# Cached values by columns: the sample group's weighted values on VectorE and ScalarE instead of TensorE

## What is computed

```python
s = einsum('bshd,bsjhd->bshj', q, kg) * scale + bias     # kg: 256 cached keys and the new one
e = exp(s - max(s));  den = sum(e)
o = einsum('bshj,bsjhd->bshd', e, vg) / den              # vg: 256 cached values and the new one
```

## Time and profile before

| | |
|---|---|
| median of 3 runs | 2500.4 us (2497.42 to 2500.45) |
| the profiled execution | 2495.72 us |
| its span | 2494.2 us |
| TensorE busy | 99% of the span |
| VectorE, ScalarE, GpSimd busy | 70%, 38%, 10% |
| mean granted TensorE clock | 0.997 |

### The profile page before, as it was taken

How to read it: one execution, slowest core, us unless ns; L and a number is a source line. 1 busy time by engine, 2 the same in 40 slices (tenths; PEclk the granted TensorE clock), 3 DMA queues, 4 the chain that set the end, 5 groups by cost and what they waited for, 6 DMA issues and landing times.

```text
span 2494.2 us, 51724 instructions
## 1 busy us (share of the span) xinstructions
PE 2465.9 (99%) x20366; PEld 2450.5 (98%) x20366; DVE 1755.0 (70%) x2203; ACT 942.2 (38%) x1225; POOL 253.0 (10%) x281
## 2 busy tenths in 40 slices
PE   8999999999999999999999999999999999999998
PEld 7999999999999999999999999999999999999998
DVE  6777787778787899888888888888433332456332
ACT  5343334333433454444444444444322221233331
POOL 1120111011100000000000000000000000143000
PEclk9999999999999999999999999999999999999999
DMA  6353333333343334433333434343665543233331
GB/s 211 119 162 104 117 109 128 112 114 105 124 145 111 135 107 149 136 118 135 118 135 118 142 121 150 124 137 120 224 208 170 164 139 120 77 93 108 110 110 68
DMA packets 99741, 324.00 MB, mean 130 GB/s; under 512 B 18258, under 2 KB 18514, under 8 KB 99168
## 3 DMA queue, kind: packets, MB, share of 16 engines
q1 hardware_dynamic: 72144, 250.25, 30.3%
q0 software_dynamic: 26672, 70.69, 8.2%
q10 hardware_dynamic: 864, 2.24, 0.2%
HBM read 286.80 MB, written 40.65 MB: 131 GB/s over the span
## 4 chain that ended last, share of the span: by engine, by line
PE 92%; DVE 3%; DMA 2%; issue 1%; ACT 1%; SPq 0%; DVEq 0%; ACTq 0%
PE acc L566 17%; PE acc L570 17%; PE acc L568 17%; PE acc L769 12%; PE acc L770 12%; PE acc L768 12%; DMA wraw<-in_w_down 1%; PE aux L615 1%; PE aux L577 1%; DMA hid<-in_x_tiles 1%; PE aux L659 1%; DVE wlo L1268 1%; DMA wraw<-in_w_in 1%; PE aux L605 0%; ACT whi L909 0%
## 5 line engine op out<-in xcount | busy, mean ns | idle before, releaser
L1268 DVE TENSOR_TENSOR wlo<-wraw,whi 128x1024 fp32r<-128x1024 f32 (+1 forms) x276 | 333.6, 1209 | 359.2 <-ACT whi L909 358.4
L909 ACT ACTIVATE whi<-wraw 128x1024 fp32r<-128x1024 f32 (+1 forms) x276 | 285.4, 1034 | 666.2 <-PE acc L570 593.2
L768 PE MATMUL acc<-xb_hi,whi 128*128 128x260 f32 x1228 | 348.3, 284 | 2.3 <-DVE xb_lo_t L1667 2.3
L770 PE MATMUL acc<-xa_hi,wlo 128*128 128x260 f32 x1228 | 349.1, 284 | 0.0
L769 PE MATMUL acc<-xa_lo,whi 128*128 128x260 f32 x1228 | 349.1, 284 | 0.0
L768 PE MATMUL acc<-xa_hi,whi 128*128 128x260 f32 x1228 | 347.4, 283 | 0.6 <-DVE wlo L1618 0.6
L770 PE MATMUL acc<-xb_hi,wlo 128*128 128x260 f32 x1228 | 347.7, 283 | 0.0
L566 PE MATMUL acc<-slots_a,whi 128*128 128x260 f32 x1536 | 312.9, 285 | 0.0
L570 PE MATMUL acc<-slots_a,wlo 128*128 128x260 f32 x1536 | 309.1, 283 | 0.0
L568 PE MATMUL acc<-slots_a,whi 128*128 128x260 f32 x1536 | 309.1, 283 | 0.0
L1085 ACT ACTIVATE whi<-wraw 128x1024 fp32r<-128x1024 f32 x176 | 186.3, 1058 | 225.0 <-PE acc L770 117.0
(11 more groups left out here) (305 smaller groups left out, 5076.9 us busy)
## 6 DMA issues: line engine op xcount, KB each, us to landing
wraw<-in_w_in SPq DMA_DIRECT2D x96, 512.0 KB, 3.6
blocks<-in_w_gate SPq DMA_DIRECT2D x88, 512.0 KB, 6.0
blocks<-in_w_up SPq DMA_DIRECT2D x88, 512.0 KB, 6.0
wraw<-in_w_down SPq DMA_DIRECT2D x48, 448.0 KB, 3.4
wraw<-in_w_out SPq DMA_DIRECT2D x32, 512.0 KB, 3.6
wraw<-in_w_ple_gate SPq DMA_DIRECT2D x32, 512.0 KB, 3.5
slots_b<-f_dram SPq DMA_DIRECT2D x28, 520.0 KB, 4.5
f_dram<-sig_t POOLq DMA_DIRECT2D x22, 520.0 KB, 3.2
```

What stands on the lines that cost most here:

```text
L768: mm(to, w_h, hi, start=p == 0, stop=False)
L770: return mm(to, w_l, hi, start=False, stop=p == KP2 - 1)
L909: on(whi[:, u % HILO, 0:width], wraw[:, u % RAW, 0:width], ACT.Copy).then_inc(s_whi, 1)
L1268: V.tensor_tensor(wlo[:, u % HILO, 0:width], wraw[:, u % RAW, 0:width], whi[:, u % HILO, 0:width].bitcast(F32), ALU.subtract).then_inc(s_w ...
```

## The change

The cached values are laid out on the host with channels on partitions (`in_cache_v`: channel, pair, token, position), and are loaded into a tile of 8 rows of 257 columns for each partition, whose last column takes the new value. The normed probabilities (16 rows of 257) are stored to DRAM and loaded back twice, each head's rows spread over its 64 partitions (`p_rows`). In step 10, at its end, VectorE multiplies the two tiles in one instruction (`sample_products`), and ScalarE sums each of the 8 rows straight into `hid` (`sample_sums`). TensorE's products and transposes of steps 7 and 9 fall away, and so do the small products, copies and sums on VectorE in steps 7, 8 and 10.

What moves with it: the key products and their sums stand one step later (2, 3 and 4 instead of 1, 2 and 3). `p_rows` shares its place with `skew`, so the next pair's `skew` is loaded once the products are done, and the next pair's keys once the sums are done. `o_low` has no tile of its own any more and uses `gate_t` (`v_t` for the last pair). ScalarE waits for the stored probabilities before it writes the keys' root over their tile. The queries' low parts stand ahead of the convolution's taps. Pair 7's products and sums stand in step 12 of the output projection.

```diff
-            if g == 7:                                       # TensorE
-                pe.wait_ge(s_row, 5 * a + 5)
-                mm(aux[:, BANK_D, KCACHE * 2 * DEC:(KCACHE + 1) * 2 * DEC], ones[0:2 * DEC, :], new_diag[:, :],
-                   start=True, stop=True)
-                for t in range(KCACHE):
-                    done = nc.tensor.transpose(aux[:, BANK_D, t * 2 * DEC:(t + 1) * 2 * DEC],
-                                               row[:, t * P:(t + 1) * P], ident[0:2 * DEC, 0:2 * DEC])
-                done.then_inc(s_str, 1)
-            if g == 9:
...
-                pe.wait_ge(s_wv, 3 * a + 3)
-                for b in range(DEC):
-                    done = mm(aux[:, BANK_D, b:b + 1], kv[:, KCACHE * b, :], ones[:, 0:1], start=True, stop=True)
-                done.then_inc(s_spv, 1)
...
+        def sample_sums(a):                                  # ScalarE
+            act.wait_ge(s_out, 3 * a + 2)
+            for b in range(DEC):
+                done = on(cached[:, b, :], cached[:, b, :], ACT.Copy, accum_out=hid[:, a, SEQ + b:SEQ + b + 1])
+            done.then_inc(s_out, 1)
...
                 if a is not None:                            # ScalarE, step 8, ahead of the keys' root
                     act.wait_ge(s_qk, 2 * j)
+                    act.wait_ge(d_p, 16 * a + 16)
                 root_of(qk_rstd, HD).then_inc(s_root, 1)
...
                 heads(j, a, g, last)                         # ScalarE, the loop over steps
+                if a is not None and g == 10:
+                    sample_sums(a)
...
-            if g == 7:                                       # VectorE
-                dve.wait_ge(s_str, 2 * a + 2)
-                V.tensor_copy(p_cols.rearrange("p t c -> p (t c)"), aux[:, BANK_D, 0:3 * 2 * DEC]).then_inc(s_pc, 1)
-                dve.wait_ge(s_pc, a + 1)
+            if g == 8:
                 dve.wait_ge(l_vc, 16 * a + 16)
-                for t in range(KCACHE):
-                    V.tensor_tensor(cached(t), cached(t), p_cols[:, t, :].rearrange("p (b e) -> p b e", b=DEC)
-                                    .unsqueeze(3).broadcast_to([P, DEC, 2, HD]), ALU.mult).then_inc(s_wv, 1)
-                dve.wait_ge(s_wv, 3 * a + 2)
-                V.tensor_tensor(cached(0), cached(0), cached(1), ALU.add).then_inc(s_wv, 1)
...
+                V.tensor_copy(cached[:, :, PAST], qkv_s[:, 2, :]).then_inc(s_out, 1)
+        def sample_products(a):
+            dve.wait_ge(l_p_rows, 32 * a + 32)
+            dve.wait_ge(s_out, 3 * a + 1)
+            V.tensor_tensor(cached[:, :, :], cached[:, :, :], p_rows[:, :, :], ALU.mult).then_inc(s_out, 1)
...
             if g == 10 and not last:                         # VectorE
                 v_lo(j)
+                q_lo(j)
                 conv_taps(j, a)
-                q_lo(j)
...
                 heads(j, a, g, last)                         # VectorE, the loop over steps
+                if a is not None and g == 10:
+                    sample_products(a)
...
-            pool.dma_start(kv[:, :, :], cache_v[0].rearrange("b (t p) h d -> p (b t) (h d)", p=P)[
-                :, :, bass.ts(a, P)]).then_inc(l_vc, 16)
+            pool.dma_start(cached[:, :, 0:PAST], cache_v[:, bass.ds(a, 1), :, :].squeeze(1)).then_inc(l_vc, 16)
+
+        def store_probs(a):
+            pool.wait_ge(s_row, 4 * a + 4)
+            apart()
+            pool.dma_start(p_dram[bass.ds(a, 1)].squeeze(0).rearrange("b e i -> (b e) i"), row[:, :]).then_inc(d_p, 16)
+
+        def load_probs(a):
+            pool.wait_ge(d_p, 16 * a + 16)
+            pool.wait_ge(s_biased, 8 * a + 8)
+            for e in range(2):
+                apart()
+                pool.dma_start(p_rows[e * HD:(e + 1) * HD, :, :],
+                               p_dram[bass.ds(a, 1), :, e, :].broadcast_to([HD, DEC, ROW_W])).then_inc(l_p_rows, 16)
...
-            pool.wait_ge(s_spv, a + 1)                       # GpSimd, attention(a)
+            store_probs(a)
+            load_probs(a)
+            if fresh:
+                store_skew(14, 16)
+                pool.wait_ge(d_skew, 16 * 4)
+            pool.wait_ge(s_out, 3 * a + 2)
             apart()
-            load_keys(a + 1)
-            if fresh:
-                store_skew(14, 16)
-            pool.wait_ge(s_biased, 8 * a + 8)
+            load_skew(a + 1)
+            pool.wait_ge(s_out, 3 * a + 3)
             apart()
-            if fresh:
-                pool.wait_ge(d_skew, 16 * 4)
-            load_skew(a + 1)
+            load_keys(a + 1)
             pool.wait_ge(s_o, 2 * a + 2)
-            pool.wait_ge(s_out, 4 * a + 4)
+            pool.wait_ge(s_out, 3 * a + 3)
             add_squares(acc_attn, hid[:, a, :], 4 * a + (SQ_X + 2))
```

More of the change, by code:

```diff
@@ L201, in build @@
     v_both = sb("v_both", [P, QB, 2, P], F32R, mix)
-    o_low = sb("o_low", [P, SEQ], scope=mix)
     u_t = sb("u_t", [P, 2 + T], scope=mix)
-    skew = sb("skew", [P, 2, SEQ], scope=mix)
+    p_rows = sb("p_rows", [P, DEC, ROW_W], scope=mix)
+    skew = p_rows.rearrange("p b i -> p (b i)")[:, 0:2 * SEQ].rearrange("p (e s) -> p e s", e=2)
     prob = sb("prob", [P, 2, SEQ], scope=mix)
@@ L208, in build @@
     stats = sb("stats", [P, 3], scope=mix)
-    kv = sb("kv", [P, DEC * KCACHE, P], scope=mix)
+    cached = sb("cached", [P, DEC, ROW_W], scope=mix)
+    kv = cached.rearrange("p b i -> p (b i)")[:, 0:DEC * PAST].rearrange("p (n f) -> p n f", f=P)
     qkv_s = sb("qkv_s", [P, 3, DEC], scope=mix)
@@ L269, in build, with o_low @@
     t_odd = tmp[:, 0:2, :].rearrange("p a t -> p (a t)").rearrange("p (n h) -> p n h", h=HALF)
+    def o_low(final):
+        return (v_t if final else gate_t)[:, 0:SEQ]
     def halves(tile):
@@ L913, in root_of, with attention @@
             return on(halves(tile[:, :]), aux_sum, ACT.Sqrt, bias=EPS, scale=1.0 / width)
-        def attention(a, g):
+        def attention(a, g, final=False):
             if 1 <= g <= 8:
@@ L925, in attention @@
                 e = (g - 5) // 4
+                if e == 0:
+                    if final:
+                        act.wait_ge(d_v, 16 * KA)
+                    else:
+                        act.wait_ge(s_conv, a + 1)
                 act.wait_ge(s_pv, 4 * a + 2 * (e + 1))
-                on(o_low[e * HD:(e + 1) * HD, :], aux[(1 - e) * HD:(2 - e) * HD, BANK_O, :], ACT.Copy).then_inc(s_olow, 1)
+                on(o_low(final)[e * HD:(e + 1) * HD, :], aux[(1 - e) * HD:(2 - e) * HD, BANK_O, :], ACT.Copy).then_inc(s_olow, 1)
             if g <= 7:
@@ L1053, in _ @@
             if 3 <= i <= PAIR_UNITS + 2:
-                attention(KA - 1, i - 3)
+                attention(KA - 1, i - 3, final=True)
+            if i == 12:
+                sample_sums(KA - 1)
             if i < KA - 1:
@@ L1289, in attention @@
                 dve.wait_ge(s_olow, 2 * a + e + 1)
-                V.tensor_tensor(hid[rows, a, 0:SEQ], aux[rows, BANK_O, :], o_low[rows, :], ALU.add).then_inc(s_o, 1)
+                V.tensor_tensor(hid[rows, a, 0:SEQ], aux[rows, BANK_O, :], o_low(final)[rows, :], ALU.add).then_inc(s_o, 1)
             if g <= 7:
@@ L1351, in attention @@
-            if g == 8:
-                V.tensor_tensor(out_s[:, :, :], qkv_s[:, 2, :].unsqueeze(2).broadcast_to([P, DEC, 2]),
-                                p_cols[:, KCACHE, :].rearrange("p (b e) -> p b e", b=DEC), ALU.mult).then_inc(s_out, 1)
[L1354 to L1358, removed]
-                V.tensor_tensor(out_s[:, :, :], out_s[:, :, :],
-                                aux[:, BANK_D, 0:DEC].unsqueeze(2).broadcast_to([P, DEC, 2]), ALU.add).then_inc(s_out, 1)
-                dve.wait_ge(s_out, 4 * a + 2)
-                for e in range(2):
-                    V.tensor_copy(hid[e * HD:(e + 1) * HD, a, SEQ:T], out_s[e * HD:(e + 1) * HD, :, e]).then_inc(s_out, 1)
@@ L1578, in _ @@
                 attention(KA - 1, i - 3, final=True)
+            if i == 12:
+                sample_products(KA - 1)
             if i < KA - 1 or i == 13:
@@ L2106, in laid_out @@
     weights["in_w_ple_proj"] = columns("w_ple_proj", PT * P)
-    return {**weights, "in_x_tiles": tiles(x), "in_p_tiles": tiles(p), "in_old_state": tiles(old),
+    values = np.ascontiguousarray(given["cache_v"][0].reshape(DEC, PAST, KA, 2, HD).transpose(3, 4, 2, 0, 1)
+                                  ).reshape(P, KA, DEC, PAST)
+    return {**weights, "in_cache_v": values, "in_x_tiles": tiles(x), "in_p_tiles": tiles(p), "in_old_state": tiles(old),
             "in_gains": np.ascontiguousarray(np.concatenate(rows).T)}
```

64 lines of the change are left out of this document (29 added, 35 removed).

## The result

The changed kernel takes 2536.95 us (median of 4 runs, 2536.41 to 2540.11), the kernel before 2498.91 us (median of 4 runs): a ratio of 1.0156, 95% interval 1.0144 to 1.0169. It is slower by 38 us. The profiled execution took 2540.11 us with a span of 2538.6 us, 44.4 us more than before by either measure. It is the slowest of its four, while the profiled execution before was as short as the fastest of the others, so the profiles differ by 6 us more than the medians.

A forecast was written before the change was run, and what follows sets the result against it. TensorE bounds the kernel, with a VectorE chain just in time behind it. Six turns at +7.2 us (+43.2), the seventh +4.7 and the last pair -1.5 give +46.4; predicted 2545 us, 8-in-10 range 2516 to 2566.

The forecast's parts named there:

- The likeliest case: VectorE's hand-off to ScalarE and back, with slow clock after each wait: 2545 us, own range 2529 to 2565; 64%.
- The second bound: In each turn, a 34.5 us chain on VectorE delivers the first probabilities only 0.05 us before TensorE takes them.
- What leaves VectorE: Steps 7 to 10: dropped small work and quieter taps bring VectorE to the end of step 10's old work 2.8 us earlier.
- What comes in: End of step 10: product 2.35 us, ScalarE's sums 3.5 us, then its split; VectorE's split starts 4.25 us later.
- Contention: GpSimd's moved squares run beside VectorE's splits and gate products, ahead of the next pair's first softmax: 0.9 us, ends 0 and 1.4.
- The clock: After each 7 us wait of TensorE the granted clock falls to 0.50, costing 2.5 us, ends 0 and 3.1.
- The seventh turn: At the convolution's output projection, VectorE's operand splits wait for ScalarE's copies behind the sums: +4.7 us, 1 of it clock.
- Covers: Row store, row loads, skew and key loads stay hidden; the skew by 2 us, the key load by over 5.
- B: Same hand-off to ScalarE and back, but the clock holds: 2529 us, from 2519 to 2539; 15%.
- D: A transfer ends last, skew or rows landing late behind the weights' loads: 3 us a turn for the skew, 2563 us; 8%.
- E: Gain and hand-off cancel, with VectorE's chain growing by 0.3 us: 2500 us; 5%.
- C: Faster, TensorE alone bounding turns: -18 us, 2482; needs VectorE's chain 1.8 us shorter, sign decided by growth under 0.45; 8%.

The follow-up runs named there:

- the kernel with both orders: Against the changed kernel: VectorE's long product put ahead of the convolution taps and ScalarE's sums behind its split of step 11; 2500.67 us, ratio 1.0007 against the kernel before.

## Why the prediction was right

The likeliest case held by its mechanism, with sizes a little too large: 2545 predicted, 2537 measured; on the footing of the profiled executions 2542 against 2540.1. The second agreement is partly luck: of the 44.4 us measured, 2.7 lie in the start stage, which the prediction did not have. Without them 41.7 us stand against the 46.4 predicted; by the medians it is 38.0.

- **The second bound.** Right. VectorE's chain sets the turn: when it was shortened step by step, the turn fell from 88.81 to 80.16 us, with the same work on TensorE. Plainest is the kernel with both orders: TensorE's work is gone there, and the turns without a fall of the clock still take 81.9 to 82.6 us, since 1.5 to 2.2 us of it come back as waiting. The last value says what the removal is worth when nothing hides it: 82.73 - 80.16 = 2.6 us a turn, where 2.29 was predicted; the 0.3 us more are not explained.
- **What leaves VectorE.** From the start of ScalarE's root to the end of step 10's old work it is 343.54 - 318.43 = 25.1 us before and 357.10 - 334.41 = 22.7 after: 2.4 us, predicted 2.8. The taps fell to 2.5 us.
- **What comes in.** The product 2.29 us (2.35 predicted), the sums 3.2 from the first one's start to the split's (3.5; 3.3 to the end of the last reading, which is the lower end of the range), VectorE's split 4.31 us later (4.25), with an idle time of 4.44. The Trainium skill's price for such a copy (ScalarE: Activation LUTs, "What ACT_TABLE_LOAD costs") is an estimated 0.40 us for 257 columns and agrees with the rows' 0.40 to 0.42. Its overlap of 93 ns between neighbours shows too: a reading starts 0.10 us before its sum ends, and the next sum 0.10 us before the reading ends. So a sum and its reading of 0.19 us cost 0.40 us together, and the prediction's 3.5 us was 0.3 too much.
- **Contention.** GpSimd's squares cost the split 1.07 us, but the norm behind it took 0.45 us where it had taken 1.09, 0.64 less: net 0.4, where 0.9 was taken. The first norm ends 36.2 us after the root's start instead of 31.4: 4.8 us later, predicted 5.15.
- **The clock.** It fell at every wait. In five recoveries the six turns lost 36.4 - 6 x (4.76 - 0.45) = 10.6 us, 2.1 each; 2.5 was taken. The sixth recovery lies in the seventh turn.
- **The sum of the six turns.** With all six recoveries 36.4 + 2.1 = 38.5 us, predicted 43.2; each of the two sizes was a little too large.
- **The seventh turn.** 7.6 - 2.1 = 5.5 us, predicted 4.7. The wait is where it was put: the first matmul of the output projection that needs the convolution's operand stood for 3.34 us. The clock fell twice there, in windows from 708 and from 742 us, where the prediction had 1 us for it. The second fall came behind two short waits, of 1.57 and 1.41 us, which the kernel before had as well without a fall; why they differ stays open.
- **The last pair** gave -1.2, predicted -1.5.
- **Covers.** No transfer was late. The skew of the turn shown was issued at 360.13 us and landed 4.3 us later, 4.3 us ahead of its first reader at 368.77, where 2 us were predicted. The view of the tile that probabilities and skew share has this line, and between 60 and 760 us VectorE's view of waits has no transfer in it:

```profile
DMA to landing us min/median/max: 3.9/6.3/10.0
```

- **The keys.** Moving them was free, by the run that moved them back.
- **The rivals.** B fell: the clock did not hold at any of the six waits. D and E fell. C was out for this kernel, because the chain grew by 4.8 us and not by less than 0.45. The argument against it, that the split cannot pass product and sums in either order, holds for the order as written only: put ahead of the sums, the split gave back 21 us. Where C's condition was made true, the sign came out, and the gain only in part: 14 us against the kernel before beside it, not 18, with 15.4 us from the six turns and 1.3 us still lost in the seventh (107.01 against 105.75). That 2482 was predicted and 2482.53 measured is luck: the prediction started from 2500.4, the kernel before took 2496.73 in that comparison.

What the prediction did not have is the start stage. In six of the eleven profiles of changed kernels the clock falls between 52 and 60 us, and their first transposes come at 103.25 to 105.80 us; in the other five it does not, and they come at 101.85 to 103.10, against 101.70 in the one profile of the kernel before. Every changed step lies behind that fall; why the clock falls in some executions stays open.

## What to carry to other kernels

Work that was taken off the busiest engine was worth nothing here until the chain behind it was shorter too; look for an engine that finishes just ahead of it (0.05 us here). When work moves to an engine that is 38% busy, its share is no argument: ask what stands behind the new work in that engine's order, and put anything that is already due, such as a weights' split, ahead of it. Moving one call behind one instruction was worth 21 us here, and the same look at each hand-off that was left turned a loss of 38 us into a gain of 14.

## What was not expected of the hardware

- In one execution waits of TensorE of 2.22 and 1.97 us were followed by the lower clock, while others of 2.44 and 1.97 us were not. A fall cost some 1.5 us there, and 2.1 us behind the long waits of the changed kernel.
- A VectorE split of 1024 columns with two SBUF inputs took 1.22 us alone and, in the rows shown, 1.84 to 2.45 beside GpSimd's products and sums of 520 columns; a norm of 128 columns took 1.07 us instead of 0.29. GpSimd's sum was slower as well, 2.15 us instead of 1.30.
- Sums along rows on ScalarE come at the price of a copy: with eight rows of 257 columns a new one starts every 0.40 us, the reading of 0.19 us included.
